# A two-model block in one launch: VectorE's and ScalarE's orders in the spatial mix, the latent attention and the experts' last outputs

## The reference, cut to what matters

```
# gMLP mixer (stages a_v, a_u, a_sv, a_g, a_out)
u, v, g = split(h @ w_in); v = layer_norm(v)              # width 2048 each
sv = einsum('gts,bcsgd->bctgd', tril(ws), v) + bs         # 16 groups, chunks of 128 tokens
h = h + (u * sv * silu(g)) @ w_out
# MLA mixer (stages m_in, m_q, m_kv, attention m, m_out)
c_q, c_kv, k_rope = split(h @ w_in)                       # 384, 256, 64
q = rms_norm(c_q) @ w_uq                                  # 8 heads, 128 + 64 rotary
k_nope, v = split(rms_norm(c_kv) @ w_ukv)                 # 8 heads, 128 + 128
o = softmax((q_nope k_nope^T + rot(q_rope) rot(k_rope)^T) * scale) v
# experts (stages pq, u, v; twice, l = 0 and 1)
q = x @ w_q; top-16 of 128 x 128 keys by head; gate = softmax(top scores)
y = sum over heads and experts of gate * gelu(u_e . x) * v_e
h = layer_norm(ALPHA * h + y)                             # l = 0: MLA follows; l = 1: the output
```

## Time and profile before

| | |
|---|---|
| time, median of 3 runs | 2340.78 us |
| the profiled execution's own time | 2340.52 us |
| its span, first to last instruction | 2338.8 us |
| mean granted TensorE clock | 0.997 |
| PE busy | 2293.7 us, 98% |
| DVE, ACT, POOL busy | 1498.4, 1166.4, 1125.4 us |
| bytes moved | 398.29 MB, 170 GB/s |

### The profile page before, as it was taken

One profiled execution on the slowest core, in us unless ns is written; L12 is line 12 of the kernel. 1 busy time (PEld: TensorE's weight loads), 2 busy tenths in 40 slices (PEclk: granted clock), 3 DMA queues, 4 the chain that ended last, 5 costly groups with the idle time before them and its releaser, 6 DMA issues. The chain is left out here.

```text
span 2338.8 us, 43269 instructions
## 1 busy us (share of the span) xinstructions
PE 2293.7 (98%) x14043; PEld 2048.9 (88%) x14043; DVE 1498.4 (64%) x3179; ACT 1166.4 (50%) x1776; POOL 1125.4 (48%) x494
## 2 busy tenths in 40 slices
PE   9999999999999999999999998999999999999998
PEld 7998989889999899988888887799999998888886
DVE  5433742331894888867777763249678887777777
ACT  5445644444555777743333344345467775443433
POOL 6867358487788666630000043478876667000000
PEclk9999999999999999999999999999999999999999
DMA  7545436355455444465556552345544445656663
GB/s 274 181 151 170 149 129 214 111 185 183 158 179 184 141 143 143 143 208 194 192 193 210 194 167 80 128 157 183 181 161 143 143 143 171 205 190 195 209 195 126
DMA packets 109593, 398.29 MB, mean 170 GB/s; under 512 B 12752, under 2 KB 13136, under 8 KB 108752
## 3 DMA queue, kind: packets, MB, share of 16 engines
q1 hardware_dynamic: 104688, 380.16, 49.0%
q10 hardware_dynamic: 4832, 17.17, 2.1%
HBM read 394.13 MB, written 3.15 MB: 170 GB/s over the span
## 5 line engine op out<-in xcount | busy, mean ns | idle before, releaser
L2112 POOL TENSOR_TENSOR w_lo<-ring,w_hi 128x1024 fp32r<-128x1024 f32 x468 | 1117.3, 2414 | 859.6 <-ACT w_hi L1007 858.9
L1007 ACT ACTIVATE w_hi<-ring 128x1024 fp32r<-128x1024 f32 x722 | 743.3, 1057 | 542.9 <-PE XX L436 387.7
L434 PE MATMUL GG<-hT_both,w_hi 128*128 128x256 f32 x1728 | 492.1, 285 | 1.5 <-DVE hT_both L1479 1.5
L436 PE MATMUL GG<-hT_both,w_lo 128*128 128x256 f32 x1728 | 488.9, 283 | 0.0
L435 PE MATMUL GG<-hT_both,w_hi 128*128 128x256 f32 x1728 | 488.8, 283 | 0.0
L544 PE MATMUL GG<-hT_both,w_hi 128*128 128x512 f32 x1152 | 410.7, 399 | 0.1
L434 PE MATMUL XX<-w_hi,hT_both 128*128 128x512 f32 x1024 | 398.7, 389 | 2.7 <-DVE w_lo L1978 2.2
L436 PE MATMUL XX<-w_hi,hT_both 128*128 128x512 f32 x1024 | 398.4, 389 | 0.0
L435 PE MATMUL XX<-w_lo,hT_both 128*128 128x512 f32 x1024 | 398.4, 389 | 0.0
L1978 DVE TENSOR_TENSOR w_lo<-ring,w_hi 128x1024 fp32r<-128x1024 f32 x248 | 304.0, 1226 | 57.0 <-ACT w_hi L1007 56.7
L434 PEld LDWEIGHTS GG<-hT_both,w_hi 128*128 128x128 f32 x1728 | 331.4, 192 | 3.1 <-issue 2.6
(11 more groups left out here) (301 smaller groups left out, 2744.1 us busy)
## 6 DMA issues: line engine op xcount, KB each, us to landing
ring<-slabs_in SPq DMA_DIRECT2D x722, 512.0 KB, 4.1
big<-rows_in ACTq DMA_DIRECT2D x10, 512.0 KB, 7.1
big<-rows_in ACTq DMA_DIRECT2D x3, 1024.0 KB, 10.3
big<-keys_in ACTq DMA_DIRECT2D x2, 1024.0 KB, 7.5
h_kept<-h ACTq DMA_DIRECT2D x2, 1024.0 KB, 11.2
h<-h_kept ACTq DMA_DIRECT2D x2, 1024.0 KB, 7.2
big<-ws_in ACTq DMA_DIRECT2D x1, 1024.0 KB, 17.5
out<-h SPq DMA_DIRECT2D x4, 256.0 KB, 2.0
```

Source lines behind the costliest of these rows:

```text
L434: nc.tensor.matmul(out, a_hi, b_hi, start=start, stop=False, skip_group_check=True)
L436: return nc.tensor.matmul(out, a_lo, b_hi, start=False, stop=stop, skip_group_check=True)
L1007: nc.scalar.activation(w_hi[:, 2 * j + half, :], ring[j][:, half * 1024:(half + 1) * 1024], ACT.Copy).then_inc(hi_ready, 1)
L2112: Q.tensor_tensor(w_lo[:, 2 * j + half, :], ring[j][:, half * 1024:(half + 1) * 1024], w_hi[:, 2 * j + half, :], ALU.subtract).then_inc(sp ...
```

## The change

1. **a_g, order.** PE does the first slab of a_g between the fourth and the fifth tile of the spatial mix; the other seven follow as straight code in place of a loop.
2. **Spatial product in PSUM.** DVE adds the bias in place in the bank, then multiplies bank by `A_u` into `A_y`, and frees the bank after that.
3. **MLA, orders.** DVE rotates the two query tiles ahead of the key, and takes only the first m_qrt tile; ACT takes the second. ACT splits m_kv's second slab after the key's copies and m_out's first slab after its m_qrt tile. The second run of keep-busy matmuls has 5 in place of 9.
4. **Attention m.** DVE's `m_rest` calls move: {3: [0], 5: [1], 7: [2, 3]}. PE's and ACT's order stays.
5. **Experts' last outputs.** For b = 1 the last four halves are done for d = 0, then again for d = 1; the halves are released in the second pass.

```diff
             for i in range(8):
+                if i == 4:
+                    project_slab(SLAB0["a_g"], 0, hT, DC, False)
                 tile = x_begin("a_sv", i)
...
-            project_cols("a_g", hT, DC)
+            for n in range(1, SLABS["a_g"]):
+                project_slab(SLAB0["a_g"] + n, 0, hT, DC, False)
...
-                for b in range(NB):
+                for j, a in ((2, 0), (2, 1), (3, 0), (3, 1)):
+                    half_ready(s0 + j, 15, a)
+                    pe.wait_ge(sem(f"gated_split{l}"), 15 * 8 + (2 * j + a + 1))
+                    for d in range(2):
+                        last = v_tile(j, a, d, False, (j, a) == (3, 1))
...
+                for d in range(2):
                     for j, a in ((2, 0), (2, 1), (3, 0), (3, 1)):
...
+                        last = v_tile(j, a, 2 + d, False, (j, a) == (3, 1))
+                        if (j, a) == (3, 1):
+                            last.then_inc(x_full, 1)
+                        elif d:
                             last.then_inc(half_done, 1)
...
-            busy_until("m_kv", 0, 9)
+            busy_until("m_kv", 0, 5)
...
-                if i % 2:
-                    split(SLAB0["m_kv"] + i // 2)
+                if i == 1:
+                    split(SLAB0["m_kv"])
             round_latents("m_ck", 0, (3, 4))
...
+            split(SLAB0["m_kv"] + 1)
...
-                if hd % 4 == 3:
-                    split(SLAB0["m_out"] + hd // 4)
+                if hd == 7:
+                    split(SLAB0["m_out"] + 1)
...
+            take_T("m_qrt", M_qrT, (1,))
+            split(SLAB0["m_out"])
...
-                y = A_y[:, 2 * i:2 * i + 2, :].rearrange("p a (b t) -> p a b t", b=NB)
-                V.tensor_tensor(y, tile[:, :].rearrange("p (a b t) -> p a b t", a=2, b=NB),
-                                bc(A_bs[:, 2 * i:2 * i + 2, :], 2, NB), ALU.add).then_inc(free, 1)
-                x_read(dve, "a_sv", i)
-                last = V.tensor_tensor(flat(A_y[:, 2 * i:2 * i + 2, :]), flat(A_y[:, 2 * i:2 * i + 2, :]),
-                                       flat(A_u[:, 2 * i:2 * i + 2, :]), ALU.mult)
-            link(last)
+                mixed = tile[:, :].rearrange("p (a b t) -> p a b t", a=2, b=NB)
+                link(V.tensor_tensor(mixed, mixed, bc(A_bs[:, 2 * i:2 * i + 2, :], 2, NB), ALU.add))
+                V.tensor_tensor(flat(A_y[:, 2 * i:2 * i + 2, :]), tile[:, :], flat(A_u[:, 2 * i:2 * i + 2, :]), ALU.mult
+                                ).then_inc(free, 1)
+            x_read(dve, "a_sv")
...
+            for i in range(2):
+                tile, free = x_tile(dve, "m_qr", i)
+                rotate_bank(tile[:, :].rearrange("p (b n d) -> p b n d", b=NB, n=4), 4, rope_row, M_tmp,
+                            [M_qr[:, :, i * 256:(i + 1) * 256].rearrange("p b (n d) -> p b n d", n=4)], sem("mq_rotated"))
+                dve.wait_ge(sem("mq_rotated"), i + 1)
+                dve.sem_inc(free, 1)
...
             kr = M_c[:, :, 640:704].unsqueeze(2)
             rotate(kr, 1, rope_row, M_tmp, sem("kr_rot"))
...
-            for i in range(2):
-                tile, free = x_tile(dve, "m_qr", i)
-                rotate_bank(tile[:, :].rearrange("p (b n d) -> p b n d", b=NB, n=4), 4, rope_row, M_tmp,
-                            [M_qr[:, :, i * 256:(i + 1) * 256].rearrange("p b (n d) -> p b n d", n=4)], sem("mq_rotated"))
-                dve.wait_ge(sem("mq_rotated"), i + 1)
-                dve.sem_inc(free, 1)
...
-            take_T("m_qrt", M_qrT, (0, 1))
+            take_T("m_qrt", M_qrT, (0,))
...
-            attention("m", False, float(P + ROPE) ** -0.5, m_unit, m_rest, VALUES_AT["m"])
+            attention("m", False, float(P + ROPE) ** -0.5, m_unit, m_rest, {3: [0], 5: [1], 7: [2, 3]})
```

More of the change, by code:

```diff
@@ L850, in experts @@
                     v_slab(j, 15, False)
-                for b in range(NB):
-                    for j, a in ((2, 0), (2, 1), (3, 0), (3, 1)):
[L853 to L861, removed]
+                for j, a in ((2, 0), (2, 1), (3, 0), (3, 1)):
[6 more added lines that the diff above has]
+                for d in range(2):
+                    for j, a in ((2, 0), (2, 1), (3, 0), (3, 1)):
+                        last = v_tile(j, a, 2 + d, False, (j, a) == (3, 1))
+                        if (j, a) == (3, 1):
+                            last.then_inc(x_full, 1)
+                        elif d:
                             last.then_inc(half_done, 1)
```

## The result

| | before | after |
|---|---|---|
| time, median (range, runs) | 2340.93 us (2340.47 to 2341.55, 4) | 2326.47 us (2325.66 to 2326.88, 4) |
| profiled execution | 2340.52 us | 2325.66 us |
| its span | 2338.8 us | 2323.9 us |

The runs of before here are those beside which the changed kernel was timed, hence 2340.93 and not 2340.78. The ratio is 0.9938, 95% interval 0.992 to 0.9955. The kernel is 14.5 us faster by the medians and 14.9 by the profiled executions.

The account below looks back on a forecast made before the run. PE, busy for 98% of the span, was taken as the bound, leaving its waits to shorten. Terms 2.8 + 3.8 + 1.4 + 0.3 + 4.2 - 0.7 = 11.8 us gave 2329.0 us, range 2326.6 to 2332.4.

Parts of the forecast that it names:

- Spatial mix, 2.8 forecast: Spatial tiles: with DVE's multiply at 0.68 us and a slab in between, waits for banks go, gaining 2.8 us.
- The 5.9 us for the first slab: Spatial mix: a_g's slab of 48 matmuls takes PE about 5.9 us, so banks are free before the fifth tile.
- the first slab's product would be late without reaching PE: a_g: DVE still owes four tiles (5.6 us) before the silu product; ACT waits, but PE has slab 2 to do.
- MLA up to m_kv, 3.8 and 1.4 forecast: Third m_qn tile: wait gone (2.28 us) and full rate (1.5), together 3.8; then m_ck's rounding and m_kv earlier by 1.4.
- First scores, 0.3 forecast: Attention's first scores: ACT doing the second copy shortens the chain of two DVE copies, gaining 0.3 us, bounds 0 and 0.7.
- Experts' last outputs, -0.7 forecast: Seam behind v0: halves released later delay ACT's rounding, root and DVE, losing 0.7 us; nothing gained at the run's end.
- 1.4 for PE's last wait: Sign in the seam behind v0: PE's wait for the transposed tokens' rest would be 1.4 us in place of 0.73.
- End of the attention, 4.2 forecast: Attention m: the 2.21 us wait before t7 goes, v3 at full rate gives 1.7, smaller gaps 0.3: 4.2 us.
- the first rival: End of attention m: v2 also runs at full rate, 1.7 us more gained, time 2327.3 us; chance 0.25.
- The meeting with POOL: Key's rotation or unit 5's normalizing is held by a POOL split, 2.1 to 2.3 us; 2331.3 to 2333.6; chance 0.12.
- The half clock did not stay at the end of the attention: Denies a rival: only the 2.2 us wait goes and v3 stays at half rate, time 2331.0 us; chance 0.13.
- The order in the bank was not slowed: Denies a rival: in-place bank work slowed by PE's writes or orders blocking, half the gain lost, 2334 to 2336; chance 0.06.

Follow-up runs that it names:

- experiment 5: Two kernels, each the kernel before plus one edit: a_g's first slab moved between spatial tiles, 2336.91 us; spatial product in PSUM, 2337.24 us.
- experiment 8: The changed kernel with nine keep-busy matmuls ahead of m_kv in place of five: 2326.11 us, ratio 0.994.
- experiment 2: The changed kernel with DVE's m_rest calls in attention m put back as before: 2331.43 us, ratio 0.9959.

## Why the prediction was right, and where it was not

**Spatial mix, 2.8 forecast, 3.33 found.** The mechanism was right, at the price given for the multiply (0.69 for 0.68), and the term 0.5 too small. It counts only the idle time. But a tile behind a pause takes 1.16 us where one in a row adds 0.92, so two pauses cost 2 x 0.24 more. The 5.9 us for the first slab don't follow from the row cited, which gives 6.3 for 48 matmuls; it took 5.6, and nothing hung on it. Item 1 alone would do. That the first slab's product would be late without reaching PE held too. What the forecast could not see in one profile is the fall of the clock behind this stall in two of four (experiment 5).

**MLA up to m_kv, 3.8 and 1.4 forecast, 3.78 and 1.45 found.** Right, step by step: no wait, the third tile at full rate, m_ck's chain earlier. One thing it could not see: the tile's half rate came in four of five profiles with that pause, so 1.5 us of this term would not come in every execution. The cut of the keep-busy matmuls, which I had priced at 1.4 - 1.06 = 0.34, is worth 0.1 by experiment 8.

**First scores, 0.3 forecast, 0.26 found.** Right.

**Experts' last outputs, -0.7 forecast, -0.71 found.** Right in size, place and sign, and the surest of all the terms (355.6 for 354.9 us in thirteen profiles). Only the sign for it was wrong: 1.4 for PE's last wait, where it is 0.86 and the loss lies ahead of the transposes. Nothing at the end: PE's last matmul starts at 2314.03 and DVE's last block at 2315.00, 0.97 apart as in the earlier trace rows.

**End of the attention, 4.2 forecast, 6.2 found.** The step that failed is "v2 itself I leave at 3.56, as the pause before it is nearly as long as now". It measured 1.89, which is 1.7 of the 2.0 us missing. The mechanism behind it, a half clock behind idle time, was right, and so was what stood around it: the pause before t6 with its cause, t7's wait gone, v3 at full rate. The pauses before t5 and t6 that it names (0.84 and 0.86) stand in none of its rows; they are in the lines under experiment 2. The size was off for two reasons. First, I took one reading, 3.56, for what these pauses always bring; over five profiles with the old order v2 ran at half rate three times and at full rate twice, so even behind the old pauses full rate had some two chances in five, not one in four. Second, the pause is not as it was. I had 1.8 to 2.0 us; it is 1.66 in one piece, between t5 and t6, with v2 right behind the transposes. Six of six profiles of the new order at full rate, against two of five, speak for a real effect of the order, though so few can't prove it. I had named this as the first rival, with 2327.3 and a chance of 0.25, which was too low, though its argument for it was itself one reading: the stretch of 1.60 us that brought no fall in that profile brought one in two of the four profiles that have it. So it is partly luck which terms of this sum came out.

**What put the median outside.** With v2 at full rate the prediction's sum is 11.8 + 1.7 = 13.5. The other 1.4 of the profiled 14.9 are 0.30 from the start of the run and 0.32 from the first experts, both untouched by the change and of the size by which executions differ (the stretch of the first experts takes 799.79 to 800.39 us over thirteen profiles), 0.53 from the spatial mix and 0.3 of the attention's smaller gaps. The bounds on the terms had reached 2326.3; the range given stopped at 2326.6.

**The rivals.** The meeting with POOL happened at unit 5 (2.61 for 0.62) and cost PE nothing, because what stood behind it had to wait for s7 until 1447.76 anyway. The prediction gives the rule of the Trainium skill (SBUF — State Buffer, section Who interferes with whom) too widely when it says that an instruction with at most one SBUF input is not held: the page excepts DVE's 2-port modes and names tensor_scalar among the operations that can enter them. The normalizing is a tensor_scalar, with one tile and a column of scalars in SBUF, and it was held; whether by such a mode or by its scalars, no run separates. The half clock did not stay at the end of the attention. The order in the bank was not slowed (0.69 to 0.70).

**The parts.** By the medians item 4 alone is worth 6.2 us, item 1 or item 2 alone 3.8 or 3.5, the query's rotation ahead 3.2, item 5 -0.9 and the shorter keep-busy run 0. 6.2 + 3.8 + 3.2 - 0.9 = 12.3, and the rest of item 3, m_ck and first scores, has 1.45 + 0.26 by the table: 14.0, against 14.5 measured. That is as close as medians that stand some tenths apart, and falls of the clock that come by chance, allow.

## What to carry to other kernels

When an in-order engine waits for a partner's result with another unit's input queued behind it, move the waiting instruction back: that costs no work, and here it was the largest part of the change. Price a pause of PE in front of the bottleneck's next work as its length plus a chance of the half clock. One profile doesn't give that chance, so read the same place in several executions, those of other kernels that share it too, and where the pause can't be removed, fill it with keep-busy matmuls (3.1 us here for two pauses). Before you blame an instruction that took long, look at when its follower could have started at all. Of two edits that remove one stall keep the simpler, and test each alone.

## What the runs showed of the hardware that I had not expected

- The granted clock behind equal pauses differs from execution to execution: 3.3 to 3.6 us or 1.97 for the same eight matmuls behind 0.84 + 0.86 + 0.21 us, 3.09 to 3.89 (four profiles) or 2.39 (one) for a tile behind 2.5 to 2.6 us, and 1.94 and 2.08 or twice 1.16 for a tile behind 1.26 + 1.60 us. A single pause of 1.66 us brought no fall in six of six. Whether the 0.25 us less in total or the one piece in place of three decides was not separated and stays open.
- The same program differs by about 2 us between two profiled executions of the changed kernel, at the start (7.50 or 8.04 us for 44 matmuls; 6.53 to 8.04 over all thirteen profiles) and in PE's waits for POOL in the first stage. How well two traces compare depends on the stretch and not on its length: 355 us up to m_in repeat within 0.04, the 800 us of the stretch before it within 0.6. So compare stretch by stretch, not from the start of the run.
- DVE instructions of two forms with their data in `big` waited when they met POOL's split: tensor-tensor (2.17 for 0.69) and tensor-scalar (2.61 for 0.62, and 3.54 for the latents' norm in both orders). With one input in a bank it was 0.68 to 0.70 while the same splits ran.
